# RET heads: q and k turned by VectorE in the first four steps, and the next head rotated ahead of the inverse roots of the current one

## The reference

```
rq = rotary(rq.reshape(B, S, 4, 256), 256, 10000.0)      # x1*cos - x2*sin, x2*cos + x1*sin
rk = rotary(rk.reshape(B, S, 4, 256), 256, 10000.0)
# per head, in two chunks of 128 rows:
scores = (q @ k.T) * decay
o = scores @ v + (q @ state) * xi
o = o * rsqrt(mean(o * o, -1) + 1e-6)                    # per row and head
o = silu(rg) * (o.reshape(B, S, 1024) * ret_norm_w)
merged = sigmoid(g_ret) * (o @ w_ret_up) + sigmoid(g_moba) * (o_moba @ w_moba_up)
```

## Time and profile before

| what | value |
|---|---|
| median of 3 runs | 2452.24 us (2452.17 to 2452.41) |
| the profiled execution's own time | 2452.33 us, of which the span in the trace is 2450.5 us |
| TensorE busy | 2443.6 us, 100% of the span |
| VectorE, ScalarE, GpSimd busy | 1525.5, 1233.7 and 228.8 us |
| chain of work that ended last | PE 98%, DVE 1%, issue 1% |
| granted TensorE clock | 1.00 |

### The profile page before, as it was taken

One profiled execution on the slowest core, in us unless ns is written; L12 is line 12 of the kernel. 1 busy time (PEld: TensorE's weight loads), 2 busy tenths in 40 slices (PEclk: granted clock), 3 DMA queues, 4 the chain that ended last, 5 costly groups with the idle time before them and its releaser, 6 DMA issues.

```text
span 2450.5 us, 35584 instructions
## 1 busy us (share of the span) xinstructions
PE 2443.6 (100%) x11789; PEld 2043.6 (83%) x11789; DVE 1525.5 (62%) x1808; ACT 1233.7 (50%) x1628; POOL 228.8 (9%) x250
## 2 busy tenths in 40 slices
PE   9999999999999999999999999999999999999999
PEld 7888888878888888888888888888887888888887
DVE  5445545587877777777777776454456645555564
ACT  6445454555455444444444445454556555655443
POOL 0021223231000000000000000010001100520000
PEclk9999999999999999999999999999999999999999
DMA  7554555566655555555555556854454545544655
GB/s 268 196 182 171 173 176 177 188 228 226 206 195 175 190 195 187 191 188 188 189 190 190 189 190 212 251 183 170 171 184 160 181 163 179 178 164 157 226 185 163
DMA packets 134819, 464.17 MB, mean 189 GB/s; under 512 B 14544, under 2 KB 21328, under 8 KB 134112
## 3 DMA queue, kind: packets, MB, share of 16 engines
q1 hardware_dynamic: 122464, 443.08, 53.6%
q10 hardware_dynamic: 12256, 20.15, 2.5%
q0 software_dynamic: 32, 0.03, 0.0%
HBM read 455.87 MB, written 7.34 MB: 189 GB/s over the span
## 4 chain that ended last, share of the span: by engine, by line
PE 98%; DVE 1%; issue 1%; ACT 0%; DMA 0%; POOL 0%; ACTq 0%; POOLq 0%; DVEq 0%
PE PS L641 21%; PE PS L643 21%; PE PS L642 21%; PE PS L890 13%; PE PS L895 7%; PE PS L917 3%; PE PS L918 3%; PE PS L919 3%; PE PS L752 1%; PE PS L723 1%; PE PS L682 1%; PE PS L703 1%; PE PS L731 0%; DVE WL L1603 0%; DMA RAW<-w_stream 0%
## 5 line engine op out<-in xcount | busy, mean ns | idle before, releaser
L1603 DVE TENSOR_TENSOR WL<-RAW,WH 128x1024 fp32r<-128x1024 f32 x842 | 1058.6, 1260 | 871.2 <-ACT WH L1099 865.2
L1099 ACT ACTIVATE WH<-RAW 128x1024 fp32r<-128x1024 f32 x841 | 889.7, 1060 | 1110.4 <-PE PS L643 725.2
L641 PE MATMUL PS<-WH,HT 128*128 128x512 f32 (+1 forms) x1816 | 720.1, 397 | 0.2 <-DVE WL L1603 0.2
L643 PE MATMUL PS<-WH,HT 128*128 128x512 f32 (+1 forms) x1816 | 706.9, 389 | 0.0
L642 PE MATMUL PS<-WL,HT 128*128 128x512 f32 (+1 forms) x1816 | 705.6, 389 | 0.0
L641 PEld LDWEIGHTS PS<-WH,HT 128*128 128x128 f32 x1816 | 341.2, 188 | 72.0 <-issue 5.3
L643 PEld LDWEIGHTS PS<-WH,HT 128*128 128x128 f32 x1816 | 340.8, 188 | 71.6
L642 PEld LDWEIGHTS PS<-WL,HT 128*128 128x128 f32 x1816 | 341.4, 188 | 66.6
L890 PE MATMUL PS<-HT,WH 128*128 128x512 f32 x1408 | 352.8, 392 | 0.0
L890 PEld LDWEIGHTS PS<-HT,WH 128*128 128x128 f32 x1408 | 253.7, 189 | 45.7
L895 PEld LDWEIGHTS PS<-HT,WL 128*128 128x128 f32 x1408 | 192.2, 190 | 13.8
(11 more groups left out here) (301 smaller groups left out, 1907.8 us busy)
## 6 DMA issues: line engine op xcount, KB each, us to landing
RAW<-w_stream SPq DMA_DIRECT2D x841, 512.0 KB, 3.3
bias_scratch<-BE ACTq DMA_DIRECT2D x12, 256.0 KB, 4.0
MEMR<-mem_in ACTq DMA_DIRECT2D x1, 2048.0 KB, 11.6
X<-x_in ACTq DMA_DIRECT2D x4, 512.0 KB, 4.4
x_scratch<-X ACTq DMA_DIRECT2D x4, 512.0 KB, 4.6
X<-x_scratch ACTq DMA_DIRECT2D x1, 2048.0 KB, 9.0
out<-X ACTq DMA_DIRECT2D x8, 256.0 KB, 3.1
X<-x_in SPq DMA_DIRECT2D x3, 512.0 KB, 9.2
```

The source lines that it names most:

```text
L641: pe.matmul(o, hi, WH[:, slot, kk, 0:cols], start=k == 0, stop=False)
L643: ins = pe.matmul(o, lo, WH[:, slot, kk, 0:cols], start=False, stop=k == nq * GK - 1)
L1099: act.activation(WH[:, g.slot(j)], RAW[:, g.slot(j)], ACT.Copy).then_inc(hi_split, 1)
L1603: dve.tensor_tensor(WL[:, s], RAW[:, s], WH[:, s].bitcast(F32), ALU.subtract).then_inc(lo_split, 1)
```

## The change

On VectorE, each of the steps 0 to 3 gets one call of `ret_turn(H, a)`: four `transpose` instructions (they turn blocks of 32 by 32) that read 32 partitions of `QK` (partitions 32a on, 256 numbers each) and write to the four groups of 32 partitions of `QKT`. After four calls all 16 blocks of both chunks of q and k stand turned in `QKT`, and `qk_tr` goes up. The layout of `QKT` is now that of `QK` (operand, row chunk, half of the width, 128), read through the view `QKR`. TensorE's transposes in step 4 and ScalarE's copies are gone; TensorE waits for `qk_tr` in step 5 in front of the scores. GpSimd rotates head 0 ahead of its loop and then, in turn `h`, rotates `h + 1` and after that takes the inverse roots of `h`. Since the rotation's scratch `JK` is then in use, ScalarE throws its squares into `PR`.

```diff
+        QKR = QKT[:].rearrange("p z c s -> p (z c s)").rearrange("p (z t c s) -> p z t c s", z=2, t=T, c=2)
...
-            with pool.Fori(0, 4) as h:
-                ch.enter(h, 2 * 5 + 1 + 1)
+            def ret_rotate(h):
                 H = At(RET0, h, 1)
                 hold(qk_tr, H.count(1))
                 for a in range(2):
...
-                hold(o_ms, At(0, h, 1).count(1))
+
+            def ret_rstd(n):
+                hold(o_ms, n.count(1))
                 link(pool.tensor_tensor(MS[:, 0:2], MS[:, 0:2], con("eps")[:, 0:2], ALU.add))
                 pool.tensor_tensor(MS[:, 0:2], MS[:, 0:2], con("half")[:, 0:2], ALU.pow).then_inc(o_rstd, 1)
-            ch.leave(4)
+            ret_rotate(0)
+            with pool.Fori(0, 3) as h:
+                ch.enter(h, 2 * 5 + 1 + 1)
+                ret_rotate(h + 1)
+                ret_rstd(At(0, h, 1))
+            ch.leave(3)
+            ret_rstd(At(3))
...
-                            ins = pe.matmul(PS[:, 6, cols], QKT[:, 1, c, s * P:(s + 1) * P], QKT[:, 0, c, s * P:S],
+                            ins = pe.matmul(PS[:, 6, cols], QKR[:, 1, s, c, :], QKR[:, 0, s:T, c, :],
...
-                st = head_steps(RET, At(RET0, i, 1), lambda s: PA[:, s, ds(i * 256 + 2 * W, 256)], (4, 5, None, 7, 10))
+                H = At(RET0, i, 1)
+                st = head_steps(RET, H, lambda s: PA[:, s, ds(i * 256 + 2 * W, 256)], (None, 5, None, 7, 10))
+                if p == 5:
+                    pe.wait_ge(head_out, H.count(1))
+                    pe.wait_ge(qk_tr, H.count(2))
+                    pe.sem_inc(qkt_ready, 1)
...
-                if p == 4:
-                    head_transpose(RET, H, None)
-                elif p == 7:
+                if p == 7:
                     act.wait_ge(pv_done, H.count(1))
-                    mean_squares([(PS[:, 4, t * 256:(t + 1) * 256], MS[:, t:t + 1]) for t in range(T)], 1 / 16.0, o_ms, JK[:])
+                    mean_squares([(PS[:, 4, t * 256:(t + 1) * 256], MS[:, t:t + 1]) for t in range(T)], 1 / 16.0, o_ms, PR[:, 0:256])
...
+            def ret_turn(H, a):
+
+                dve.wait_ge(qk_fixed, H.count(1))
+                src, dst = [tile.rearrange("p z u s -> p (z u s)").rearrange("p (n s) -> p n s", s=P) for tile in (QK[:], QKT[:])]
+                for b in range(4):
+                    ins = dve.transpose(dst[32 * b:32 * b + 32, :, 32 * a:32 * a + 32], src[32 * a:32 * a + 32, :, 32 * b:32 * b + 32])
+                if a == 3:
+                    ins.then_inc(qk_tr, 1)
+
             def ret_step(i, p):
-                st = head_steps(RET, At(RET0, i, 1), None, i, lambda t: PA[:, t, ds(i * 256 + 3 * W, 256)], (5, 8, 10))
+                H = At(RET0, i, 1)
+                if p < 4:
+                    ret_turn(H, p)
+                st = head_steps(RET, H, None, i, lambda t: PA[:, t, ds(i * 256 + 3 * W, 256)], (5, 8, 10))
```

## The result

The changed kernel takes 2455.88 us (median of 20 runs, 2454.90 to 2457.33) against 2452.22 us (20 runs, 2451.69 to 2452.41). The ratio is 1.0016, 95% interval 1.001 to 1.0022. So it is slower by 3.7 us. The forecast was 2456.0 us, slower by 3.7 us, inside the band of 0.2% (4.9 us) that counted as no change. The size came out right, but the waits in heads 1 to 3 had been put too high and the fall of TensorE's clock, which stood as a rival, made up for it.

A forecast was written before the change was run, and what follows sets the result against it. The prediction took TensorE's row of instructions to bound the kernel (busy 2443.6 of 2450.5 us). Its terms, -3.5 + 3.7 + 0.5 + 2.6 + 0.4, add +3.7 us to 2452.33 us: 2456.0 us, range 2451.0 to 2458.3.

The forecast's parts named there:

- Removed transposes: TensorE, step 4: dropping eight transposes saves 0.88 us a head, -3.5 us over four heads.
- The 275 ns for each: TensorE's 32 removed transposes at the skill's price: worth 8.8 us, total 2450.7 us; chance 0.02.
- Length and distance of VectorE's transposes: VectorE, steps 0 to 3: each transpose lasts 0.44 us, 0.47 with no overlap, 1.88 us a step.
- overlapping neighbours: Rival on VectorE: transposes overlap at 0.35 us each, head 0 waits 1.5 us, total 2451.2 us; chance 0.12.
- Head 0's wait: TensorE before head 0's scores: qk_tr comes at 354.3, wanted at 350.61, so it waits 3.7 us.
- Heads 1 to 3: TensorE before these heads' scores: waits for qk_tr of 0.16 us a head, 0.5 us in all.
- Inverse roots: GpSimd's roots come late behind a 15.1 us rotation; TensorE waits 0.86 us in heads 0, 1 and 2: 2.6 us.
- rival 1: GpSimd's rotation takes 14.2 us, inverse roots are in time, the 2.6 us go: 2453.3 us; chance 0.15.
- Weight loads: TensorE: loads left uncovered by four clear waits, about 0.1 us each, an estimated 0.4 us.
- The clock: Rival: TensorE's clock falls in head 0's wait, slow matmuls cost 1.8 us more: 2457.8 us; chance 0.13.
- one row of a harmless wait: Sign that short waits spare TensorE's clock: a 1.1 us wait is followed by four matmuls in 1.16 us, 0.26 apart.
- The sum: Whole kernel: -3.5 + 3.7 + 0.5 + 2.6 + 0.4 us, that is +3.7 us, 2456.0 us.

The follow-up runs named there:

- e6_small_turns: The changed kernel with each of a head's 16 transposes on 128 partitions by 64 columns, so q and k are not transposed: 2448.87 us.
- e3_no_silu: The changed kernel without the Silu over PA in front of the loop, so VectorE's first split came 2.0 us earlier: 2452.69 us.
- e2_roots_first: The changed kernel with GpSimd's old order, inverse roots of head h before the rotation of head h + 1: 2457.03 us.
- e7_roots_between: The changed kernel with GpSimd's inverse roots of head h between the q and k halves of the next head's rotation: 2454.39 us.
- the spread kernel: The changed kernel with a head's first eight transposes in steps 9 and 10 of the turn before, the others in steps 0 and 1: 2449.60 us.
- e5_dummies: The changed kernel with four matmuls, whose result nobody reads, in front of TensorE's wait for the turned q and k: 2456.88 us.
- e4_step_later: The changed kernel with the head's work from the scores on one step later: 2452.24 us, with one of ten runs at 4102.93 us.

## Why the prediction was right, and where it was not

- *Removed transposes, -3.5 us.* Right: -3.3 us with all waits gone (e6_small_turns), -3.7 by the scores' distance. The 275 ns for each that the Trainium skill gives ("TensorE: Matmul & The Clock Gate", section "Part 4: PE-mode transpose"), -8.8 us in all, is out: by it e6_small_turns would have taken 2443.4 us, and it took 2448.87.
- *Length and distance of VectorE's transposes, 0.44 and 0.47 us.* Right, 0.436 and 0.445. The distance was the step that decided: by the 0.35 of overlapping neighbours head 0 would have waited 1.5 us in place of 3.5, and the rotations of the others would have started 2.2 us earlier, with their inverse roots in time. The Trainium skill's rule of held instructions ("VectorE: DVE Perf Modes", section "Two Vector instructions with no wait between them") agrees with the traces: 0.445 apart where partitions change, 0.13 apart at a length of 0.21 where they don't.
- *Head 0's wait, 3.7 us.* Right, 3.5 (TensorE would have begun at 350.57, as in e6_small_turns, and began at 354.09); e3_no_silu shows that it follows VectorE's start.
- *Heads 1 to 3, 0.5 us.* Too high: nothing. Sixteen transposes at 0.445 in place of 0.47 are 0.4 us less, so the last one of head 1 ends at 391.39, 0.2 us before the scores start.
- *Inverse roots, 2.6 us.* The mechanism is right (e2_roots_first, e7_roots_between), the size was off. Heads 1 and 2 waited for 0.74 and 0.71 us (16.28 us from scores to output before, 17.02 and 16.99 now), and head 0 for nothing, since the slow clock held TensorE itself up by more than that. 1.45 in place of 2.6. Head 0's rotation took the 14.2 us of rival 1, but its roots were late all the same, since the operation behind it met a split (1.63 us). Where the clock stays up, head 0's wait appears (three of them in e3_no_silu).
- *Weight loads, 0.4 us.* The size is right: the starts are later by 3.52, 0.74 and 0.71 us at idle times of 3.39, 0.56 and 0.53 in the trace, 0.49 more in all. It is part of the delays named above. That it is weight loads no run shows.
- *The clock, a rival with 0.13.* It happened. From scores to output head 0 took 18.01 us against 16.29, so the fall cost 1.7 us; the price worked out was 1.8. The rival added it to a wait for the roots in head 0, which it hides, so the fall makes the kernel only about 1.0 us slower (2455.88 against 2454.90). In all but one of the 20 runs the mean granted clock is 0.999, and the one with 1.000 is the fastest, 2454.90 us. The prediction has no reason against a fall in head 0; its one row of a harmless wait is 1.1 us long and speaks for the short waits alone. The 0.13 stood on no row with a wait as long, and the fall came in 19 of 20 runs.
- *The sum.* -3.7 + 3.5 + 1.7 + 1.5 = +3.0 us in the stretch by the trace (the removed transposes by the scores' distance), 3.3 by the spans, 3.7 by the medians. What is outside the span grew from 1.8 to 2.1 us in the profiled executions, as in every kernel with the change; the cause of that 0.3 stays open.

The forecast named the right places. That its total came so close is in part luck: 1.7 us of clock stand where 0.5 for the transposes of heads 1 to 3 and 1.5 of the waits for roots (2.6 against idle times of 1.1) had been put too much.

## What to carry to other kernels

When work moves off the bounding engine, add up all that the new one has to do between the moment at which it can begin and the moment at which the output is wanted; here that was 12.1 us of work in a gap of 12.3, and in the first turn of the loop 12.1 in 8.7. The input was there before that: the spread kernel, which began on it in the turn before, has no wait for it. A gain of 0.9 us a head was lost to the one head for which the helper started late, and a wait of 2.5 us or more on TensorE was paid again in slow matmuls in most runs. In-order engines make a queue of unrelated work: before a long operation is put in front of a short one, look who waits for the short one, and cut the long one in two if it can't go elsewhere.

## What the runs showed of the hardware that I had not expected

- TensorE's clock fell to 1.2 GHz with waits of 2.5 and 3.4 us (inside the wait, 0.4 us before its end, in e5_dummies; 0.15 us behind it in the changed kernel) and was back within 3.6 us of the next matmul, but not in every execution: after the same wait of 3.4 us it stayed at 2.4 GHz in the profiled execution of e2_roots_first. The kernels with such a wait spread over 1.0 to 2.5 us (e7_roots_between and e2_roots_first), the changed kernels without it over 0.5 to 1.1 (but for the one run of e4_step_later), and the kernel before over 0.7 to 2.1 in sets of 20 to 33 runs; how much of the spread is the clock's no run shows, for in e7_roots_between, the narrowest, it fell in all ten. The Trainium skill warns of gaps between bursts ("TensorE: Matmul & The Clock Gate", section "Why this matters for your kernels"), and the traces agree, except that the fall did not come every time.
- GpSimd's second operation of the inverse roots, two columns wide, took 1.63 us instead of 0.71 in head 0, where a split of VectorE had started 0.16 us before it (368.65 and 368.81). It ended 0.56 us behind the end of that split, and so it did in e6_small_turns; in head 1 of e4_step_later, where it began 0.33 us after a split's start, it ended 0.57 behind. Even an operation of two columns waits until the split is over.
